# Uneven token chunks, 388, 388 and 256 in place of three of 344, through a whole decoder step on one core

## The reference

```python
def swiglu(h, wg, wu, wd):
    return (jax.nn.silu(h @ wg) * (h @ wu)) @ wd
...
for layer in range(DEPTH):                      # DEPTH = 2
    h = rmsnorm(x, p["mix_norm"][layer])
    if layer < N_A_LAYERS:                      # layer 0: S5 state space, GELU, GLU
        y, hr, hi = s5_mixer(h, ...)            # out = (z @ w_ga) * sigmoid(z @ w_gb)
    else:                                       # layer 1: differential attention
        k = rope_partial(kv_in @ w_k); v = kv_in @ w_v; q = rope_partial(h @ w_q)
        y = rmsnorm(attend(q, k, v, pos, lam)) * (1 - lam_init) @ w_o
    x = x + y
    x = x + swiglu(rmsnorm(x, ffn_norm), gate, up, down)    # 1024 -> 2816 -> 1024
return rmsnorm(x, final_norm), k, v, states
```

## Time and profile before

| what | us |
|---|---|
| median of 3 runs (2397.66 to 2401.24) | 2399.03 |
| the profiled execution's own time | 2399.81 |
| its span in the profile | 2398.0 |
| PE busy | 2322.8 |
| PEld busy | 2246.0 |
| DVE busy | 1544.4 |
| ACT busy | 844.6 |
| POOL busy | 913.5 |

### The profile page before, as it was taken

One profiled execution on the slowest core, in us unless ns is written; L12 is line 12 of the kernel. 1 busy time (PEld: TensorE's weight loads), 2 busy tenths in 40 slices (PEclk: granted clock), 3 DMA queues, 4 the chain that ended last, 5 costly groups with the idle time before them and its releaser, 6 DMA issues.

```text
span 2398.0 us, 40617 instructions
## 1 busy us (share of the span) xinstructions
PE 2322.8 (97%) x16134; PEld 2246.0 (94%) x16134; DVE 1544.4 (64%) x2427; ACT 844.6 (35%) x1592; POOL 913.5 (38%) x621
## 2 busy tenths in 40 slices
PE   7889999999999999999999999999999999999998
PEld 6779999999999999999999866689999999999997
DVE  9993247766665676476534677765866656566746
ACT  4442134333333324232100377753433333342423
POOL 0003335555555545532332100042555555545550
PEclk9999999999999999999999999999999999999999
DMA  3145111222222514212257355210122222251422
GB/s 124 40 124 193 40 32 45 103 92 103 92 104 80 180 42 159 98 56 95 89 171 226 111 143 145 62 51 30 56 103 86 99 92 103 80 186 53 142 89 71
DMA packets 125495, 239.04 MB, mean 100 GB/s; under 512 B 36346, under 2 KB 80890, under 8 KB 125314
## 3 DMA queue, kind: packets, MB, share of 16 engines
q1 hardware_dynamic: 103634, 186.29, 24.4%
q10 hardware_dynamic: 21680, 50.22, 5.7%
HBM read 178.13 MB, written 55.98 MB: 98 GB/s over the span
## 4 chain that ended last, share of the span: by engine, by line
PE 79%; DVE 14%; issue 2%; ACT 2%; DMA 1%; POOL 1%; SPq 0%; DVEq 0%; ACTq 0%; POOLq 0%
PE pair L2415 30%; PE pair L2669 16%; PE pair L2673 15%; PE pair L2672 15%; DVE act_lo L1535 2%; PE pair L2937 1%; DVE w_lo L1535 1%; DVE X L1535 1%; DVE nmx L2218 1%; DVE act_lo L1616 1%; DVE Vp L1535 1%; DMA zn<-zblk 1%; DVE wmix L2295 1%; DVE mixed L1535 1%; DVE acc L1535 1%
## 5 line engine op out<-in xcount | busy, mean ns | idle before, releaser
L2669 PE MATMUL pair<-act_hi,w_hi 128*128 128x344 f32 x1920 | 615.4, 321 | 4.2 <-DVE act_lo L1616 2.8
L2673 PE MATMUL pair<-act_hi,w_lo 128*128 128x344 f32 x1920 | 614.0, 320 | 0.0
L2672 PE MATMUL pair<-act_lo,w_hi 128*128 128x344 f32 x1920 | 612.9, 319 | 0.0
L2415 PE MATMUL pair<-act_hi,w_hi 128*128 128x344 f32 x1152 | 372.0, 323 | 2.7 <-DVE act_lo L1535 2.1
L2415 PE MATMUL pair<-act_hi,w_lo 128*128 128x344 f32 x1152 | 368.9, 320 | 0.0
L2415 PE MATMUL pair<-act_lo,w_hi 128*128 128x344 f32 x1152 | 368.5, 320 | 0.0
L2669 PEld LDWEIGHTS pair<-act_hi,w_hi 128*128 128x128 f32 x1920 | 360.7, 188 | 6.5 <-DVE act_lo L1616 2.1
L2673 PEld LDWEIGHTS pair<-act_hi,w_lo 128*128 128x128 f32 x1920 | 360.9, 188 | 0.0
L2672 PEld LDWEIGHTS pair<-act_lo,w_hi 128*128 128x128 f32 x1920 | 360.3, 188 | 0.0
L1535 DVE TENSOR_TENSOR w_lo<-w_raw,w_hi 128x512 fp32r<-128x512 f32 (+1 forms) x242 | 231.9, 960 | 117.8 <-ACT w_hi L985 115.5
L843 POOL TENSOR_TENSOR w_lo<-w_raw,w_hi 128x512 fp32r<-128x512 f32 x120 | 165.8, 1381 | 356.4 <-ACT w_hi L990 356.4
(11 more groups left out here) (328 smaller groups left out, 4159.0 us busy)
## 6 DMA issues: line engine op xcount, KB each, us to landing
w_raw<-w SPq DMA_DIRECT2D x180, 512.0 KB, 4.4
act_raw<-hid SPq DMA_DIRECT2D x20, 688.0 KB, 6.2
hid<-gate ACTq DMA_DIRECT2D x22, 516.0 KB, 2.7
hid<-gate_odd ACTq DMA_DIRECT2D x22, 516.0 KB, 2.7
mix<-mixes_of ACTq DMA_DIRECT2D x16, 688.0 KB, 5.1
mixed_f<-mix SPq DMA_DIRECT2D x12, 688.0 KB, 6.4
kpg<-cache_k SPq DMA_DIRECT2D x16, 512.0 KB, 5.2
vpg<-cache_v SPq DMA_DIRECT2D x16, 512.0 KB, 8.1
```

The lines of the kernel that those rows point to most:

```text
L2415: return t_.matmul(out, lhsT, rhs, start=start, stop=stop)
L2669: ins = t_.matmul(out, wh, rhs[k][0], start=first and k == 0, stop=False, skip_group_check=True)
L2672: t_.matmul(out, wh, rhs[k][1], start=False, stop=False, skip_group_check=True)
L2673: last = t_.matmul(out, wl, rhs[k][0], start=False, stop=k == HK - 1, skip_group_check=True)
```

## The change

The chunks become 388, 388 and 256 tokens wide in every stage. Chunks 0 and 1 are the two that the seven products join; chunk 2 has the four plain products. The number of instructions stays, but for `roots` and `diagonals`, where one ACT root becomes two and one reciprocal and one diagonal become two each, since the blocks of a quarter chunk are 97 or 64 wide. Tiles with a chunk axis become flat over the 1032 tokens, some places in SBUF move, and `pair_lo0` shares the place of `sq`.

```diff
-CW = T // NC
-TB = CW // 4
+TBS = (97, 97, 64)
+CWS = tuple(4 * x for x in TBS)
+CW = CWS[0]
+OFF = (0, CW, 2 * CW)
...
-        pair_lo0 = place("pair_lo0", [P, T], F32R)
...
+        top[0] = max(top[0], HID_AT + 24 * CW * 4)
         MISC_AT = top[0]
...
+        flat_sq = nc.alloc_sbuf_tensor_at("flat_sq", [P, T], F32, offset=MISC_AT)
+        pair_lo0 = nc.alloc_sbuf_tensor_at("pair_lo0", [P, T], F32R, offset=MISC_AT)
-        acc = place("acc", [P, NC, CW], F32, misc)
+        acc = place("acc", [P, T], F32, misc)
...
-        tmp = place("tmp", [P, 4, CW], F32, misc)
-        gate = place("gate", [P, NC, CW], F32, misc)
+        tmp = place("tmp", [P, T + CW], F32, misc)
+        gate = place("gate", [P, T], F32, misc)
...
         def cs(n):
-            return slice(n * CW, (n + 1) * CW)
+            return slice(OFF[n], OFF[n] + CWS[n])
+
+        def psum(i, n):
+            return bank[i][:, 0:CWS[n]]
...
             def roots(v):
                 act.wait_ge(nm_ss, 3 * v + 3)
-                a.activation(std[0:TB].rearrange("p n j -> p (n j)"), bank[7][0:TB, 0:4 * NC], ACT.Sqrt,
-                             scale=1.0 / DM, bias=eps_t[0:TB, :]).then_inc(nm_std, 3)
+                for first, last in ((0, 2), (2, 3)):
+                    tb = TBS[first]
+                    a.activation(std[0:tb, first:last].rearrange("p n j -> p (n j)"), bank[7][0:tb, 4 * first:4 * last], ACT.Sqrt,
+                                 scale=1.0 / DM, bias=eps_t[0:tb, :]).then_inc(nm_std, last - first)
...
             def diagonals(v):
                 dve.wait_ge(nm_std, 3 * v + 3)
-                c.step(v_.reciprocal(rstd[0:TB], std[0:TB]))
-                W12 = [TB, 4 * NC, TB]
-                tt(sq[0:TB].rearrange("p n (j t) -> p (n j) t", j=4), bc(ident[0:TB, 0:TB], 1, W12),
-                   bc(rstd[0:TB].rearrange("p n j -> p (n j)"), 2, W12), ALU.mult).then_inc(nm_diag, 3)
+                parts = ((0, 2), (2, 3))
+                for first, last in parts:
+                    tb = TBS[first]
+                    c.add(v_.reciprocal(rstd[0:tb, first:last], std[0:tb, first:last]))
+                c.sync()
+                for first, last in parts:
+                    tb, m = TBS[first], 4 * (last - first)
+                    WM = [tb, m, tb]
+                    tt(flat_sq[0:tb, OFF[first]:OFF[first] + m * tb].rearrange("p (m t) -> p m t", m=m), bc(ident[0:tb, 0:tb], 1, WM),
+                       bc(rstd[0:tb, first:last].rearrange("p n j -> p (n j)"), 2, WM), ALU.mult).then_inc(nm_diag, last - first)
...
             def block(f, b, w, beside):
                 B = NBK * f + b
-                x1, x3, x2, cg, cu = (bank[(5 * b + i) % 8][:, 0:CW] for i in range(5))
+                x1, x3, x2, cg, cu = (psum((5 * b + i) % 8, 2 if i > 2 else 0) for i in range(5))
...
-                    v_.scalar_tensor_tensor(stage[:, slot + x, cs(n)], bank[b + x][:, 0:CW], scale, R[:, cs(n)],
+                    v_.scalar_tensor_tensor(stage[:, slot + x, cs(n)], psum(b + x, n), scale, R[:, cs(n)],
```

More of the change, by code:

```diff
@@ L184, in build @@
         rstd = place("rstd", [P, NC, 4], F32)
-        diag = place("diag", [TB, 4, TB], F32)
+        diag = place("diag", [TBS[0], CW], F32)
         sel = place("sel", [P, HC], F32)
@@ L1729, in block @@
                 dve.wait_ge(st_ev, n8 + 3)
-                tt(U[:, 1, :], x3, u3, ALU.add).then_inc(st_ev, 1)
+                tt(U[:, cs(1)], x3, u3, ALU.add).then_inc(st_ev, 1)
                 dve.wait_ge(st_ev, n8 + 4)
@@ L1779, in mixes @@
                 dve.wait_ge(mx_dve, done)
-                tt(one, even[:, 1, :], even[:, 0, :], ALU.subtract).then_inc(mx_dve, 1)
-                tt(three, odd[:, 1, :], even[:, 1, :], ALU.subtract).then_inc(mx_dve, 1)
+                tt(one, even[:, cs(1)], even[:, cs(0)], ALU.subtract).then_inc(mx_dve, 1)
+                tt(three, odd[:, cs(1)], even[:, cs(1)], ALU.subtract).then_inc(mx_dve, 1)
                 dve.wait_ge(mx_dve, done + 1)
-                tt(two, one, odd[:, 1, :], ALU.subtract).then_inc(mx_dve, 1)
+                tt(two, one, odd[:, cs(1)], ALU.subtract).then_inc(mx_dve, 1)
                 dve.wait_ge(mx_dve, done + 3)
-                tt(four, odd[:, 0, :], two, ALU.add).then_inc(mx_dve, 1)
+                tt(four, odd[:, cs(0)], two, ALU.add).then_inc(mx_dve, 1)
             def refill_low(f, b, name):
@@ L1802, in down_block @@
                 n8, added = 8 * B, 3 * (ND * f + b - FT)
-                x1, x3, x2, cg, cu = (bank[(5 * b + i) % 8][:, 0:CW] for i in range(5))
-                p1, u2 = tmp[:, 3, :], part[:, 0, :]
+                x1, x3, x2, cg, cu = (psum((5 * b + i) % 8, 2 if i > 2 else 0) for i in range(5))
+                p1, u2 = tmp[:, T:], part[:, 0, :]
                 def into_x(m, n, out, counted):
@@ L2392, in out_pair @@
                     o = X[:, 2 * p + x, cs(n)]
-                    tt(o, o, bank[2 * n + x][:, 0:CW], ALU.add).then_inc(op_added, 1)
+                    tt(o, o, psum(2 * n + x, n), ALU.add).then_inc(op_added, 1)
                 for x in range(2):
@@ L2468, in first_pairs @@
                         pe.wait_ge(counted, done(s - 3))
-                    out = [bank[2 * (s % 3) + x][:, 0:CW] for x in range(2)]
+                    out = [psum(2 * (s % 3) + x, n) for x in range(2)]
                     last = dense(out[0], (u + 2 * t) % 4, n, act_hi, act_lo, s in (0, 5))
@@ L2479, in pair_of_units @@
             def pair_of_units(n, u, ready, beside={}, release=True, arrive=None):
-                last = dense(bank[2 * n][:, 0:CW], u % 4, n, act_hi, act_lo, n == 0 and release, arrive)
+                last = dense(psum(2 * n, n), u % 4, n, act_hi, act_lo, n == 0 and release, arrive)
                 if n == NC - 1:
@@ L2613, in product @@
                     ah, al = act_hi[:, k, cs(n)], act_lo[:, k, cs(n)]
-                    out = bank[2 * n + x][:, 0:CW]
+                    out = psum(2 * n + x, n)
                     ins = mm(out, wh, ah, k == 0, False)
```

112 lines of the change are left out of this document (60 added, 52 removed).

## The result

The changed kernel took 2400.72 us (median of 20 runs, 2397.34 to 2406.17), the kernel before 2398.27 beside it (20 runs): 1.0013 [1.0007, 1.0019] (ratio, with its 95% interval, as everywhere below). By the medians it is 2.4 us slower, inside the 0.2% that was called no change; the forecast was 2388.5, faster. Its profiled execution has a span of 2402.8 us.

What follows compares the result with a forecast made beforehand. TensorE (PE) was taken to bound the kernel, without idle time in the filled blocks. Streaming -13.2, entries +2.0, refills +0.5 and tail 0 summed to -10.7 us, so 2388.5 us, range 2381 to 2406.

Steps and rivals of the forecast that it cites:

- Streaming: Matmuls of the 60 feed-forward blocks: 528 fewer columns streamed per block, -13.2 us.
- the other reading: Matmul step: the extra time grows with the columns, step 0.4575 N, giving -14.5 us over 60 blocks.
- the constant extra: Matmul step: the same 14.0 ns on top of N/2.4 for each matmul, giving -13.2 us; the reading taken.
- The weight load's floor: Rival: 256-column matmuls on chunk 2 hit the weight load, slower; 2407 us (chance 0.12) or about 2434 (0.05).
- the pair of sums for the ends: Costs of longer operations at the feed-forward entries, +2.0 us, and in the down projection's refills, +0.5 us.
- entries: Start of each feed-forward, where PE waits for VectorE's longer work: +2.0 us, at most 3.2 for both.
- refills: Down projection's weight refills, 4.3% more columns, nearly all beside PE: +0.5 us, between 0 and 3.2.
- Plain stages: Stages running alike over all three chunks: two chunks' longer steps cancel the third's shorter ones, 0 us.
- Tail: After the last long matmul: shorter final operations against VectorE falling behind, sum 0, between -1.2 and +1.1 us.
- Moving tiles: Tiles moved in SBUF and flat views issue no instructions: priced at nothing.
- the stages' ends eat the gain: Rival: entries, refills and tail cost in full, leaving -5.7 us; 2393 us, up to 2398 with new waits; chance 0.13.

Runs made afterwards that it cites:

- e8: Changed kernel with four edits of work order, two at the feed-forwards' entries and two in their first refill turns: 2395.86 us, 0.9990 of the kernel before.
- e9: Changed kernel's code with equal chunks of 344 columns and the same four edits of order as e8: 0.9991 of the kernel before.

## Why the prediction was wrong

*Streaming, -13.2:* right in kind and size. It measured -14.4. That this meets the other reading's -14.5 is in part luck, since the two kernels stand at different places: at one and the same place the table gives -17.6, -14.4, -13.6 and -13.2. The steps don't settle the two readings either. From 256 to 388 columns they rise by 0.439 to 0.450 ns a column at the four places, between the 0.4167 of the constant extra and the 0.4575 of the other. The forecast itself is off by 0.2 us: 2399.03 - 10.7 is 2388.3.

*The weight load's floor, 0.17 in all:* refuted by the step of 118.0 ns, which is what the columns ask for and under the 123.2 from which that rival would have decided. The Trainium skill ("TensorE: Matmul & The Clock Gate", LDWEIGHTS) gives an estimate of 106.7 ns for the load, and the trace agrees in so far as 118.0 shows no floor.

*The step that failed is the pair of sums for the ends.* They were priced as the widened operations at the waits that PE already had: entries +2.0 with a bound of 3.2, refills "nearly all is beside PE, so I take +0.5" with a bound of 3.2. They measured +5.0 for the entries, and for the refill turns +5.7, +7.0 with the last blocks. Two things were missed. VectorE has next to no idle time in the first turn, and little at the entry, so there each operation of the longer chunk moves the end, adds into `X` included, and ScalarE's queue moves it too (the silu behind a refill's transfer). The prediction says under its rival that VectorE is full in these stretches, and still takes its added work as lying beside PE. e8 took 5.5 us of it back by order alone; the rest is read from the waits, no run removed it. And a stretch that another chain paces can't pass on PE's shorter steps: the forecast counted 0.22 us for each of 60 blocks, those of the entries and turns as well. This second point is argued from the ledger, no run shows it by itself.

*Plain stages, 0:* the matmuls are right (+0.6), but PE's waits at their seams cost 1.8 more.

*Tail, 0:* the parts came out as told. The four final multiplications took 2.48 us for 3.21, the spread 0.70 for 0.85, and VectorE fell behind by 0.88 (from the last matmul's start to the last add 1.24 us in place of 0.36; forecast 1.1). Timeline of the changed kernel's end, beside the earlier trace rows:

```profile
2394.56 0.70 PE L2438 MATMUL pair<-diag,ones 64*128 64x256 f32 x2 [1.00 <-DVE diag L1550]
2395.29 2.48 DVE L1550 TENSOR_TENSOR Y<-X,pair 128x512 f32<-128x512 f32 x4 [0.79 <-PE pair L2438]
```

What came beside it is the store, which ends 5.0 us after these multiplications and ended 4.3 after them before.

*Moving tiles, "at nothing":* wrong in kind. The changed kernel's place, 32 modulo 128, is as good as the old one for equal chunks, but not for the new widths: its block takes 20.553 us there and 20.500 at the old place, 3.2 us in 60 blocks (1.9 by the times, within the intervals). At 344 columns place 96 was worth 5 us.

The rival that came true is "the stages' ends eat the gain", priced at -5.7 us "and up to 2398 if new waits appear": right in kind, and even its upper end 3 us too low.

## What to carry to other kernels

When a change shortens the engine that bounds the filled part and lengthens the operations of the others, price it per column on both sides: here a column brought 0.33 to 0.40 us in 60 blocks, by the place of the operands, and cost about as much at the entries, turns and seams, so neither of the two widths tried won in the given order of work. In a stretch where a second engine shows no idle time, count its whole lengthened chain, and count nothing of the first engine's gain. Before a change that moves tiles is judged, run its code with the old sizes: here that run was as fast as any, and without it the place's share would have been put down to the widths or to the order.

## What the runs showed of the hardware

The matmul's step depends on where its operands stand in SBUF. With the same matmuls the block of 132 took 20.793, 20.793, 20.753 and 20.733 us at the four places modulo 128 bytes, and 20.500 to 20.553 with the other widths. At each of the 132 positions the step repeats within 0.5 ns over 36 blocks (standard deviation; the records are in whole ns), and lies between 152 and 164 ns for 344 columns. Shifts of 1024 and 4096 bytes leave every step as it was within 0.3 ns; whether the period is 128 bytes or another divisor of 1024 wasn't tried. The weights `w_hi` and `w_lo` stand ahead of `act_hi` and moved in none of these runs, so it is the place of the activations, by itself or beside that of the weights, that sets the steps. The Trainium skill ("SBUF — State Buffer", Specifications (TRN2)) has lines of 16 bytes, each new one at a price; the shifts here are whole such lines, so that alone doesn't explain it.

A subtraction of VectorE's from SBUF to SBUF takes longer while GpSimd works: 0.68 us alone and 1.31 beside it for 128x512 (kernel before), 1.58 alone and 3.72 beside it for 128x1376 (kernel before and e9).
